# Context maxima of the next head pair: moved from four places in two units into four consecutive rounds of one unit

## The chip, the cores and the metric

The kernel runs on one core of a Trainium2 chip. The metric is the device time of one execution in microseconds (us), lower is better. All work is in one program; its stages follow one another with a barrier between them.

## The reference, cut to what matters

Two transformer layers over 1024 latent tokens and a prefix of 256 context tokens. In each layer 16 heads (8 of latent attention "MLA", 8 of grouped-query attention "GQA") attend; latent queries see all 1280 keys. In the first layer the context tokens attend too, over the 256 context keys alone; in the last layer they don't, since the context stream isn't used any more.

```python
o = jnp.concatenate([
    blocked_attention(qm, jnp.concatenate([kmc, km], axis=1),
                      jnp.concatenate([vmc, vm], axis=1), MLA_SCALE),
    blocked_attention(qg, jnp.concatenate([kgc, kg], axis=1),
                      jnp.concatenate([vgc, vg], axis=1), GQA_SCALE)], axis=-1)
x = layer_norm(ALPHA * x + ga * (o @ w_o[l]), ln1_g[l], ln1_b[l])
if not last:
    oc = jnp.concatenate([blocked_attention(qmc, kmc, vmc, MLA_SCALE),
                          blocked_attention(qgc, kgc, vgc, GQA_SCALE)], axis=-1)
# blocked_attention: softmax over the keys of q.k * scale, times v, per block of 128 queries
```

## The kernel before, in words

The function `attention` (L851) is one stage per layer. It walks through a list `U` of units. A unit is a pair of heads and a group of queries: (pair, first tile, tiles, key tiles). In the first layer each of the 8 pairs has three units: one context unit (2 query tiles, 2 key tiles), then two latent units (4 query tiles and all 10 key tiles each). Unit numbers run 0 to 23; units 0, 3, 6, ..., 21 are context units, 1, 4, ... are here called the first latent unit of a pair and 2, 5, ... the second. In the last layer there are no context units. Pairs 0 to 3 are MLA, pairs 4 to 7 GQA.

A unit works in rounds `k`, one for each key tile. In a round TensorE computes transposed scores (`scores`, L1096; keys on the partitions; 6 matmuls for MLA, 4 for GQA), ScalarE takes the exponential (`exponential`, L1177), and VectorE adds the result into a running sum (`accumulate`, L1233). The weighted values (`values`, L1123) are held back and issued in bunches: those of two rounds at k = 2, of three at k = 5, of three at k = 8, the last two at k = 0 of the next unit (`held`, L938).

The exponential needs the maximum of each query's row beforehand. It enters the scores as an extra row of the query operand, so it must be known before the unit begins. For each query tile and head of a *later* unit there is therefore an extra score matmul with the queries on the partitions, `begin(v, s)` (L1061), into a PSUM area, and VectorE takes the negated maximum of it (`maximum`, L1228, instruction L1231). For a latent unit that is 3 matmuls over 1280 keys and a reduction of 1280 columns; for a context unit one matmul over 256 keys and a reduction of 256 columns. A latent unit needs 8 of these, a context unit 4 (s = 0 to 3). When all are there, `turn(v)` (L1088) transposes the maxima, ScalarE copies them out (`take_row`, L1199) and SyncE's queue copies them into the query operand (`set_row`, L1011).

After the prologue all `begin`s share one PSUM area, `at_sc`: each waits until the maximum before it has been read out:

```python
if n >= PRO:
    pe.wait_ge(max_done, n)      # L1071, in begin; n is this begin's number in the whole order
```

In which round each `begin` is issued is written out by hand. `ahead(u, k)` gives those of later latent units: one in each round 0 to 5 and 8, 9. `context_ahead(u, k)` gives those of the next context unit: s = 0 and 1 in rounds 2 and 5 of the first latent unit before it, s = 2 and 3 in rounds 2 and 5 of the second. The order in a round on TensorE is: `scores(u, k)`, the `turn`s of `turned` (round 6), the `begin`s of `ahead`, the last values and sums of the unit before (rounds 0 and 1), the held `values`, and then the `begin` of `context_ahead` (L1155 to L1169). On VectorE it is: the maximum of `ahead`, `accumulate`, the maximum of `context_ahead`, and `invert` (L1255 to L1264). `invert(w)` takes the reciprocal of the softmax sums of an earlier unit, which went out to DRAM and came back by GpSimd's DMAs. TensorE and VectorE take their instructions in this written order.

The tables `begun`, `T_BEFORE`, `A_NO` (L913 to L924) follow from the two functions, so that both engines agree on the numbers to wait for. The maxima of the first two units of the stage are computed in its prologue and are in neither function.

Of the kernel before, what the change touches and what calls it, by code (L numbers as in the profile page):

```python
# [25 lines left out]
CT = CTX // P  # L26
LT = SEQ // P
NT = CT + LT
# [822 lines left out]
def attention(nc, S, C, layer):  # L851
# [17 lines left out]
    U = []  # L869
# [5 lines left out]
    LATENT = [u for u in range(len(U)) if U[u][3] == NT]  # L875
# [4 lines left out]
    def place(u):  # L880
        return U[u] + (U[u][2] * P,)

    def ahead(u, k):

        if U[u][3] != NT:
            return []
        n = LATENT.index(u)
        if k < 6 and n + 1 < len(LATENT):
            return [(LATENT[n + 1], k + 2)]
        if k >= 8 and n + 2 < len(LATENT):  # L890
            return [(LATENT[n + 2], k - 8)]
        return []

    def context_ahead(u, k):

        if U[u][3] != NT or k not in (2, 5):
            return []
        for v, half in ((u + 2, 0), (u + 1, 2)):
            if v < len(U) and U[v][3] == CT:
                return [(v, half + (k == 5))]  # L900
        return []

    def turned(u, k):

        if U[u][3] != NT:
            return []
        n = LATENT.index(u)
        if k == 6 and n + 1 < len(LATENT):
            return ([u + 1] if U[u + 1][3] == CT else []) + [LATENT[n + 1]]
        return []  # L910

    early = [0, 1] if first_layer else [0]
    begun = [(v, s) for v in early for s in range(2 * U[v][2])] + [(LATENT[1], s) for s in range(2)]  # L913
    T_BEFORE = {(v, s): early.index(v) for v in early for s in range(2 * U[v][2])}
    T_BEFORE.update({(LATENT[1], s): len(early) for s in range(2)})
    turns = list(early)
    for u in range(len(U)):
        for k in range(U[u][3]):
            turns += turned(u, k)
            begun += ahead(u, k) + context_ahead(u, k)  # L920
            T_BEFORE.update({vs: len(turns) for vs in ahead(u, k) + context_ahead(u, k)})
    A_NO = {vs: n for n, vs in enumerate(begun)}
    T_NO = {v: n for n, v in enumerate(turns)}
    assert len(A_NO) == len(begun) == sum(2 * unit[2] for unit in U) and len(T_NO) == len(U)  # L924
# [21 lines left out]
    with ExitStack() as cx:  # L946
# [35 lines left out]
        def score_bank(n):  # L982

            return st[:, :, :, :].rearrange("p b h n -> p (b h n)") if n < PRO and n % 2 else sc
# [75 lines left out]
        def _(pe):  # L1060
            def begin(v, s):  # L1061

                pair, t0, na, kb, nq = place(v)
                a, h, n = s // 2, s % 2, A_NO[v, s]
                if s == 0:
                    pe.wait_ge(q_loaded[v % QR][0], 16 * (v // QR + 1))
                    if pair < G0:
                        pe.wait_ge(k_loaded[pair % 2][0], 16 * (pair // 2 + 1))
                    else:
                        pe.wait_ge(g_loaded[0], 16)  # L1070
                if n >= PRO:  # L1071
                    pe.wait_ge(max_done, n)
                elif n >= 2:
                    pe.wait_ge(max_done, n - 1)
                bank = score_bank(n)
                if T_BEFORE[v, s]:
                    pe.wait_ge(nm_out, T_BEFORE[v, s])
                if pair < G0:
                    qq, kk = q[0:QK, v % QR, 0, a, h, :], km[0:QK, pair % 2, 0, h, :]
                else:  # L1080
                    qq, kk = q[:, v % QR, 0, a, h, :], kg[:, (pair - G0) // 2, :]
                for lo, hi in SC:
                    if lo < kb * P:
                        hi = min(hi, kb * P)
                        ins = nc.tensor.matmul(bank[:, lo:hi], qq, kk[:, lo:hi], start=True, stop=True)  # L1085
                ins.then_inc(a_full, 1)

            def turn(v):  # L1088

                na = U[v][2]  # L1090
                pe.wait_ge(max_done, A_NO[v, 2 * na - 1] + 1)
                if T_NO[v]:
                    pe.wait_ge(nm_out, T_NO[v])
                nc.tensor.transpose(sc[0:2 * na, 1280:1408], nm[:, v % 3, 0:2 * na], C["ident"][:, :]).then_inc(nm_full, 1)
# [28 lines left out]
            def values(u, k):  # L1123

                pair, t0, na, kb, nq = place(u)
                j = AT[u] + k
                if j == 0:
                    pe.wait_ge(v_loaded, 16)
                if k == 0 and u > 0:
                    pe.wait_ge(den_taken, u)  # L1130
                pe.wait_ge(exp_done, j + 1)
                for h in range(2):
                    col = 2 * pair + h if pair < G0 else H_MLA + (pair - G0) // 2
                    ins = nc.tensor.matmul(op[VD * h:VD * h + VD, 0:nq], va[:, k, col * VD:(col + 1) * VD],  # L1134
                                           pt[:, j % PT, h, 0:nq], start=(k == 0), stop=(k == kb - 1))
                ins.then_inc(v_done, 1)

            def sums(u):

                nq = U[u][2] * P  # L1140
                pe.wait_ge(acc_done, sums_done(u))
                pe.wait_ge(op_taken, u + 1)
                for h in range(2):
                    ins = nc.tensor.matmul(op[VD * h:VD * h + VD, 0:nq], C["ones"][:, 0:VD], acc[:, u % 2, h, 0:nq], start=True, stop=True)
                ins.then_inc(r_full, 1)
# [8 lines left out]
            for u in range(len(U)):  # L1154
                for k in range(U[u][3]):  # L1155
                    scores(u, k)
                    for v in turned(u, k):
                        turn(v)
                    for v, s in ahead(u, k):
                        begin(v, s)  # L1160
                    if k == 0 and u > 0:
                        for i in range(U[u - 1][3] - 2, U[u - 1][3]):
                            values(u - 1, i)
                    if k == 1 and u > 0:
                        sums(u - 1)
                    for i in held(u, k):
                        values(u, i)
                    for v, s in context_ahead(u, k):
                        begin(v, s)  # L1169
            u = len(U) - 1  # L1170
            for i in range(U[u][3] - 2, U[u][3]):
                values(u, i)
# [53 lines left out]
        @block.vector  # L1226
        def _(dve):
            def maximum(v, s):  # L1228
                kb = U[v][3]
                dve.wait_ge(a_full, A_NO[v, s] + 1)  # L1230
                nc.vector.tensor_reduce(nm[:, v % 3, s:s + 1], score_bank(A_NO[v, s])[:, 0:kb * P], AX.X, ALU.max, negate=True).then_inc(max_done, 1)  # L1231

            def accumulate(u, k):  # L1233
                nq = U[u][2] * P
                j = AT[u] + k
                out = acc[:, u % 2, :, 0:nq]
                dve.wait_ge(exp_done, j + 1)
                if k == 1:
                    if u >= 2:
                        dve.wait_ge(r_full, u - 1)  # L1240
                    before = pt[:, (j - 1) % PT, :, 0:nq]
                else:
                    dve.wait_ge(acc_done, sums_done(u - 1) + k - 1)
                    before = out
                nc.vector.tensor_tensor(out, before, pt[:, j % PT, :, 0:nq], ALU.add).then_inc(acc_done, 1)  # L1245

            def invert(u):

                dve.wait_ge(dc_loaded, 16 * (u + 1))
                n = 2 * U[u][2] * P // RC  # L1250
                nc.vector.reciprocal(rc[0:n, u % 2, :], dc[0:n, u % 2, :]).then_inc(inv_done, 1)

            for v, s in begun[:PRO]:
                maximum(v, s)
            for u in range(len(U)):  # L1255
                for k in range(U[u][3]):
                    for v, s in ahead(u, k):
                        maximum(v, s)
                    if k > 0:
                        accumulate(u, k)  # L1260
                    for v, s in context_ahead(u, k):
                        maximum(v, s)
                    for w in inverted(u, k):
                        invert(w)  # L1264
            u = len(U) - 1
            nq = U[u][2] * P
            dve.wait_ge(r_full, u + 1)
            dve.wait_ge(ot_ready, u - 1)
            nc.vector.reciprocal(rinv[:, u % 2, 0:nq], op[:, 0:nq]).then_inc(inv_done, 1)
            dve.wait_ge(inv_done, u + 1)  # L1270
            dve.wait_ge(op_taken, u + 1)
            dve.wait_ge(o_stored[u % 2], 16 * (u // 2))
            dve.wait_ge(ot_ready, u)
            nc.vector.tensor_tensor(ot[:, u % 2, 0:U[u][2], :].rearrange("p a n -> p (a n)"), raw[:, u % 2, 0:nq],
                                    rinv[:, u % 2, 0:nq], ALU.mult).then_inc(ot_ready, 1)
# [1026 lines left out]
```

## Time and profile before

| what | value |
|---|---|
| time, median of 3 runs | 3781.95 us (3776.68 to 3788.75) |
| the profiled execution's own time | 3788.75 us |
| its span in the profile | 3787.0 us |
| attention stage of the first layer | from about 445 us to 999 us of the span |
| granted TensorE clock, mean | 0.936 of full speed |

The profile is a page with the busy time of each engine, a strip of the span in 40 slices, the DMA queues, the chain that ended last, and the costliest groups of instructions. Besides it the trace can be asked for waits, for instructions in order of time, and for the busy time of chosen stretches. PE is TensorE's matmul row, PEld its weight loads; a row of PE that isn't idle can still be a matmul draining, because ends of matmuls are modelled. The start of a weight load (PEld) is the better mark of when TensorE came to the next piece of work.

### The profile page before, as it was taken

The numbers are of one execution on the slowest core, as the hardware profiler recorded it, in microseconds if no ns is written. First come the engines' busy times: TensorE is split into PE (matmuls) and PEld (weight loads), VectorE is DVE, ScalarE is ACT, GpSimd is POOL, SyncE is SP. The second block draws the span as 40 slices with busy tenths as digits, with TensorE's granted clock in tenths as the row PEclk, the third lists the DMA queues.
The fourth block names the chain that finished last, engine by engine and source line by source line (L and its number), as shares of the span: only waits on it lengthen the run. The fifth ranks groups of instructions, "written<-read, shape, count | busy, mean of one in ns | idle before, by whom it ended". The sixth has DMA issues, their size and how long they took to land. (4 is left out here: it accounts for less than half of the span.)

```text
span 3787.0 us, 44337 instructions
## 1 busy us (share of the span) xinstructions
PE 3304.8 (87%) x14416; PEld 2224.1 (59%) x14416; DVE 2715.6 (72%) x2841; ACT 1853.9 (49%) x2125; POOL 1456.2 (38%) x1091
## 2 busy tenths in 40 slices
PE   6999699999695999999959996999978599999990
PEld 2555355544384788888824443555437488887870
DVE  1444466677586899989856654777767698988997
ACT  0222233344310888888823332333331188888881
POOL 2111011121111877777721110111121287777771
PEclk9999799999896999999979997999999699999995
DMA  8465532211441998798754336221115278997974
GB/s 339 157 233 186 157 94 67 58 48 37 143 150 71 404 365 309 275 350 321 298 210 135 124 102 181 73 64 43 40 39 196 98 292 336 349 363 284 353 276 195
DMA packets 258758, 739.56 MB, mean 195 GB/s; under 512 B 55456, under 2 KB 149440, under 8 KB 205272
## 3 DMA queue, kind: packets, MB, share of 16 engines
q0 software_dynamic: 114288, 528.57, 36.4%
q1 hardware_dynamic: 129816, 157.73, 13.7%
q10 hardware_dynamic: 14544, 51.92, 3.8%
q8 instruction: 53, 0.87, 0.1%
q14 instruction: 57, 0.47, 0.0%
HBM read 723.62 MB, written 129.61 MB: 225 GB/s over the span
## 5 line engine op out<-in xcount | busy, mean ns | idle before, releaser
L2033 DVE TENSOR_TENSOR ex_wl<-ex_wr,ex_wh 128x2048 fp32r<-128x2048 f32 x440 | 988.0, 2285 | 63.9 <-ACT ex_wh L1978 63.8
L1978 ACT ACTIVATE ex_wh<-ex_wr 128x2048 fp32r<-128x2048 f32 x440 | 843.1, 1916 | 77.4 <-PE ex_yp L1941 55.1
L1185 ACT ACTIVATE at_pt<-at_st 128x1024 f32<-128x1024 f32 (+1 forms) x336 | 336.5, 1003 | 552.7 <-PE at_st L1120 550.0
L1231 DVE TENSOR_REDUCE at_nm<-at_sc 128x1 f32<-128x1280 f32 (+1 forms) x276 | 378.3, 1371 | 216.1 <-PE at_sc L1085 213.6
L764 PE MATMUL zp<-w_in,hT 128*128 128x480 f32 x960 | 428.8, 580 | 31.5 <-DVE hT L539 21.6
L1245 DVE TENSOR_TENSOR at_acc<-at_acc,at_pt 128x1024 f32<-128x1024 f32 x256 | 318.2, 1243 | 94.6 <-ACT at_pt L1185 92.4
L1859 POOL DMA_INDIRECT ex_wr<-in_w_down,piece_of x152 | 315.6, 2077 | 46.3 <-issue 46.0
L1134 PE MATMUL at_op<-at_pt,at_va 128*64 128x512 f32 (+1 forms) x1344 | 318.6, 603 | 0.2
L1120 PE MATMUL at_st<-at_q,at_km 96*128 96x512 f32 (+3 forms) x1008 | 266.2, 404 | 16.6 <-DMA at_q<-at_nmT 14.6
L764 PEld LDWEIGHTS zp<-w_in,hT 128*128 128x128 f32 x960 | 173.5, 195 | 180.2 <-issue 168.5
L1120 PEld LDWEIGHTS at_st<-at_q,at_km 96*128 96x128 f32 (+1 forms) x1008 | 180.6, 193 | 104.0 <-issue 42.6
L1879 POOL DMA_INDIRECT y_s<-ex_y,row_to x72 | 192.8, 2677 | 120.2 <-ACT ex_y L1986 117.3
L1918 PE MATMUL ex_gp<-ex_wh,ex_xh 128*128 128x512 f32 x576 | 226.7, 394 | 13.3 <-DVE ex_wl L2033 13.3
L1859 POOL DMA_INDIRECT ex_wr<-in_w_gate,piece_of x152 | 219.7, 1445 | 46.5 <-issue 46.5
L1936 PE MATMUL ex_yp<-ex_wh,ex_hh 128*128 128x512 f32 x576 | 233.3, 405 | 0.1
L1937 PE MATMUL ex_yp<-ex_wl,ex_hh 128*128 128x512 f32 x576 | 228.7, 397 | 0.0
L1919 PE MATMUL ex_gp<-ex_wl,ex_xh 128*128 128x512 f32 x576 | 226.2, 393 | 0.0
L1920 PE MATMUL ex_gp<-ex_wh,ex_xl 128*128 128x512 f32 x576 | 225.3, 391 | 0.0
L1920 PE MATMUL ex_vp<-ex_wh,ex_xl 128*128 128x512 f32 x576 | 224.3, 389 | 0.0
L1918 PE MATMUL ex_vp<-ex_wh,ex_xh 128*128 128x512 f32 x576 | 224.1, 389 | 0.0
L1919 PE MATMUL ex_vp<-ex_wl,ex_xh 128*128 128x512 f32 x576 | 224.1, 389 | 0.0
L1852 POOL DMA_INDIRECT ex_xb<-h_s,row_from x76 | 197.2, 2595 | 24.3 <-issue 22.5
(281 smaller groups left out, 5941.2 us busy)
## 6 DMA issues: line engine op xcount, KB each, us to landing
ad_w<-in_w_ada POOLq DMA_DIRECT2D x48, 1024.0 KB, 10.4
q_mla<-qT SPq DMA_DIRECT2D x40, 384.0 KB, 3.8
k_mla<-kT SPq DMA_DIRECT2D x40, 384.0 KB, 5.7
at_km<-k_mla SPq DMA_DIRECT2D x16, 960.0 KB, 12.0
at_q<-q_mla SPq DMA_DIRECT2D x32, 384.0 KB, 11.6
w_in<-in_w_in SPq DMA_DIRECT2D x6, 1920.0 KB, 25.5
q_gqa<-gqT SPq DMA_DIRECT2D x20, 512.0 KB, 6.8
cy<-y_s POOLq DMA_DIRECT2D x10, 1024.0 KB, 7.1
```

The costliest lines, as they stand in the source:

```text
L764: ins = nc.tensor.matmul(zp[:, n, 0:ZW], hT[:, k, :], w_in[:, k, n * ZW:(n + 1) * ZW], start=(k == 0), stop=(k == KC - 1))
L1120: ins = nc.tensor.matmul(st[:, j % 2, h, 0:nq], kk, qq, start=(m == 0), stop=(m == len(passes) - 1))
L1134: ins = nc.tensor.matmul(op[VD * h:VD * h + VD, 0:nq], va[:, k, col * VD:(col + 1) * VD], pt[:, j % PT, h, 0:nq], start=(k == 0), stop=(k ...
L1185: nc.scalar.activation(pt[:, j % PT, :, 0:nq], st[:, j % 2, :, 0:nq], ACT.Exp).then_inc(exp_done, 1)
L1231: nc.vector.tensor_reduce(nm[:, v % 3, s:s + 1], score_bank(A_NO[v, s])[:, 0:kb * P], AX.X, ALU.max, negate=True).then_inc(max_done, 1)
L1245: nc.vector.tensor_tensor(out, before, pt[:, j % PT, :, 0:nq], ALU.add).then_inc(acc_done, 1)
L1859: pool.indirect_dma_start(wr[:, u, p].rearrange("p a n -> p (a n)"), None, w, bass.IndirectOffsetOnAxis(R["wi"][:, p % 2, b:b + 1], 0), bo ...
L1918: nc.tensor.matmul(out[:, :], xh[:, k, :], wh[:, q, j, :], start=(k == 0), stop=False)
L1919: nc.tensor.matmul(out[:, :], xh[:, k, :], wl[:, q, j, :], start=False, stop=False)
L1920: ins = nc.tensor.matmul(out[:, :], xl[:, k, :], wh[:, q, j, :], start=False, stop=(k == KC - 1))
L1978: nc.scalar.activation(wh[:, q], wr[:, u, p], ACT.Copy).then_inc(hi_done, 1)
L2033: nc.vector.tensor_tensor(wl[:, q], wr[:, u, p], wh[:, q].bitcast(F32), ALU.subtract).then_inc(lo_done, 1)
```

## The change

`context_ahead` and its two loops go. `ahead` now also gives the context unit's `begin`s: in rounds 2, 3, 4, 5 of the second latent unit of a pair, s = 0, 1, 2, 3 of the context unit that follows, each right behind the latent `begin` of the same round. On VectorE the context maximum comes right behind the latent one and ahead of `accumulate`. There are seven such context units (3, 6, ..., 21) with 28 `begin`s and 28 maxima; nothing is added or removed in number. The last layer's attention has no context unit and the same order as before.

```diff
         n = LATENT.index(u)
         if k < 6 and n + 1 < len(LATENT):
-            return [(LATENT[n + 1], k + 2)]
+            return [(LATENT[n + 1], k + 2)] + ([(u + 1, k - 2)] if k >= 2 and U[u + 1][3] == CT else [])
         if k >= 8 and n + 2 < len(LATENT):
             return [(LATENT[n + 2], k - 8)]
-        return []
-
-    def context_ahead(u, k):
-
-        if U[u][3] != NT or k not in (2, 5):
-            return []
-        for v, half in ((u + 2, 0), (u + 1, 2)):
-            if v < len(U) and U[v][3] == CT:
-                return [(v, half + (k == 5))]
         return []
...
-            begun += ahead(u, k) + context_ahead(u, k)
-            T_BEFORE.update({vs: len(turns) for vs in ahead(u, k) + context_ahead(u, k)})
+            begun += ahead(u, k)
+            T_BEFORE.update({vs: len(turns) for vs in ahead(u, k)})
...
                     for i in held(u, k):
                         values(u, i)
-                    for v, s in context_ahead(u, k):
-                        begin(v, s)
...
                     if k > 0:
                         accumulate(u, k)
-                    for v, s in context_ahead(u, k):
-                        maximum(v, s)
                     for w in inverted(u, k):
                         invert(w)
```

## Rows read from the trace of the kernel before

**Rows 1.** The page: busy time, share, count of each engine; clock in 40 slices.

```profile
PE 3304.8 (87%) x14416; PEld 2224.1 (59%) x14416; DVE 2715.6 (72%) x2841; ACT 1853.9 (49%) x2125; POOL 1456.2 (38%) x1091
...
PEclk9999799999896999999979997999999699999995
```

**Rows 2.** Waits, 500 to 995 us: total us, times, longest.

```profile
ACT at_pt L1185 <- PE at_st L1120: 263.8, 148, 7.4
...
DVE at_nm L1231 <- PE at_sc L1085: 81.1, 68, 2.8
...
PE at_sc L1085 <- DVE at_nm L1231: 15.4, 32, 1.4
```

**Rows 3.** Timeline, second latent unit of an MLA pair (unit 5), rounds 2 to 6.

```profile
585.46 0.65 PEld L1085 LDWEIGHTS at_sc<-at_km,at_q 96*128 96x128 f32 x3
...
586.35 1.94 PE L1134 MATMUL at_op<-at_pt,at_va 128*64 128x512 f32 x8
586.46 1.49 DVE L1231 TENSOR_REDUCE at_nm<-at_sc 128x1 f32<-128x1280 f32 x1 [0.56 <-PE at_sc L1085]
...
588.22 0.19 PEld L1085 LDWEIGHTS at_sc<-at_km,at_q 96*128 96x128 f32 x1 [0.81 <-DVE at_nm L1231]
...
589.61 0.64 PEld L1085 LDWEIGHTS at_sc<-at_km,at_q 96*128 96x128 f32 x3
...
592.14 0.53 PEld L1085 LDWEIGHTS at_sc<-at_km,at_q 96*128 96x128 f32 x3 [0.60 <-DVE at_nm L1231]
...
592.72 1.24 PEld L1120 LDWEIGHTS at_st<-at_q,at_km 97*128 97x128 f32 x6
593.14 1.48 DVE L1231 TENSOR_REDUCE at_nm<-at_sc 128x1 f32<-128x1280 f32 x1
594.54 1.21 DVE L1245 TENSOR_TENSOR at_acc<-at_acc,at_pt 128x1024 f32<-128x1024 f32 x1
594.67 0.53 PEld L1085 LDWEIGHTS at_sc<-at_km,at_q 96*128 96x128 f32 x3 [0.71 <-DVE at_nm L1231]
...
598.19 0.19 PEld L1085 LDWEIGHTS at_sc<-at_km,at_q 96*128 96x128 f32 x1 [0.81 <-issue]
...
598.30 1.23 PEld L1120 LDWEIGHTS at_st<-at_q,at_km 97*128 97x128 f32 x6
598.62 0.42 DVE L1231 TENSOR_REDUCE at_nm<-at_sc 128x1 f32<-128x256 f32 x1 [0.33 <-PE at_sc L1085]
...
599.58 0.08 PEld L1094 LDWEIGHTS at_sc<-c_ident,at_nm 128*4 128x4 f32 x1
```

**Rows 4.** Timeline, second latent unit of a GQA pair (unit 14), rounds 2 to 6.

```profile
789.02 0.66 PEld L1085 LDWEIGHTS at_sc<-at_kg,at_q 128*128 128x128 f32 x3
...
795.48 0.53 PEld L1085 LDWEIGHTS at_sc<-at_kg,at_q 128*128 128x128 f32 x3 [1.08 <-DVE at_nm L1231]
...
801.62 0.19 PEld L1120 LDWEIGHTS at_st<-at_q,at_kg 128*128 128x128 f32 x1
...
802.44 0.09 PEld L1094 LDWEIGHTS at_sc<-c_ident,at_nm 128*4 128x4 f32 x1
```

**Rows 5.** Timeline, first latent units (units 7, 13), around round 3.

```profile
629.39 0.85 PE L1085 MATMUL at_sc<-at_km,at_q 96*128 96x512 f32 x3 [1.39 <-DVE at_nm L1231]
...
763.12 0.42 DVE L1231 TENSOR_REDUCE at_nm<-at_sc 128x1 f32<-128x256 f32 x1
...
763.59 0.84 PE L1085 MATMUL at_sc<-at_kg,at_q 128*128 128x512 f32 x3
```

**Rows 6.** Stretches of one unit (4, 7, 14, 17): us, busy times, PEclk.

```profile
549.34:581.12 31.78, 30.50 (x132) 17.98 (x133) 24.07 (x22) 11.14 (x13) 7.05 (x12) 1.00 0.33 80
...
617.58:652.92 35.34, 33.62 (x132) 18.78 (x133) 23.70 (x22) 11.14 (x13) 6.82 (x12) 0.90 0.32 76
...
785.59:813.78 28.19, 25.59 (x110) 13.56 (x111) 21.73 (x19) 11.34 (x14) 4.47 (x8) 1.00 0.13 36
847.72:877.46 29.74, 27.11 (x110) 14.18 (x111) 21.84 (x19) 11.35 (x15) 4.68 (x8) 0.94 0.10 28
```

## The prediction, made before the changed kernel was run

> **What bounds the kernel now.** I read the page first. TensorE is the busiest engine, VectorE the second [rows 1], but that is an average over stages, and the change touches one stage only, the first layer's attention (445 to 999 us). So the waits of that stage come next [rows 2]: ScalarE waited 263.8 us for scores and VectorE 81.1 us for TensorE, while matmuls of `begin` waited 15.4 us in all for VectorE. TensorE therefore sets the pace of the stage, and every microsecond in which it stands still there is lost. Then the timeline of a second latent unit, the place of the change, in an MLA pair [rows 3] and in a GQA pair [rows 4]. I call the latent `begin` of round k A(k) and a context `begin` B.
>
> The reader should see two things there. First, one score area is handed back and forth: from A(4)'s weight load at 592.14 VectorE starts its reduction 1.00 later (593.14), needs 1.48, and A(5) loads 0.05 behind its end, at 594.67. So **two `begin`s in a row cannot stand closer than 2.53 us** when the first is a latent one, whatever else TensorE has to do. In rounds 3 and 4 of the MLA unit that loop is already the pace (592.14 to 594.67, with scores between them that fill only part of it). Second, in rounds 2 and 5 B costs nearly nothing, because the held values stand between A and B: A(2) loads at 585.46, the reduction runs from 586.46 to 587.95, and meanwhile TensorE works on values from 586.35 until B loads at 588.22. B itself takes 0.11 of TensorE (598.19 to 598.30) and 0.42 of VectorE.
>
> **The change part by part.** It removes no instruction and adds none, and moves no DMA: 28 Bs, each one matmul over 256 keys, are issued elsewhere. 14 leave the first latent units; 14 stay in the second ones but in front of the values; so all 28 now stand right behind an A and wait for its reduction. Behind the waiting B on TensorE's queue stand the held values in rounds 2 and 5 and the next round's scores in rounds 3 and 4; ScalarE waits for those scores. SyncE's queue of row copies waits for the `turn` in round 6, which only moves with the rest; GpSimd's chain of sums goes on during the stalls and comes out no later.
>
> *MLA-type second units (2, 5, 8, 11; four).* From A(2) to the `turn` in round 6 now: 585.46 to 599.58, 14.12 us [rows 3]. In the changed order:
> - Round 2: A and its wait 2.53, B 0.11, then the values. These take 588.22 − 585.46 − 0.65 (A's own loads) = 2.11 with the gap ahead of them. Sum 4.75, where it is 2.87 now (585.46 to 588.33): +1.88.
> - Rounds 3 and 4: 2.53 + 0.11 + scores 1.28 (598.30 to 599.58) = 3.92 against 2.53: +1.39 each. B's reduction is through 0.43 + 0.42 + 0.05 = 0.90 after B's load (598.19 to 598.62, then 0.42) [rows 3], under the scores' 1.28, so A(k+1) doesn't wait for it.
> - Round 5: values and gap 598.19 − 594.67 − 0.64 = 2.88; 2.53 + 0.11 + 2.88 = 5.52 against 3.63: +1.89.
>
> Together +6.55 a unit, **26.2 us** for four.
>
> *GQA-type second units (14, 17, 20; three).* The span from A(2) to the `turn` is 789.02 to 802.44, 13.42 us [rows 4]. Scores take 0.82 (801.62 to 802.44). In the changed order: round 2 2.53 + 0.11 + 2.11 + 0.82 = 5.57; rounds 3 and 4 2.53 + 0.11 + 0.82 = 3.46, but VectorE has reduction 1.48, B's latency and reduction 0.85 and `accumulate` 1.21 in a row, which makes the next reduction about 0.1 late, so 3.55; round 5 2.53 + 0.11 + 2.88 + 0.82 = 6.34. Sum 19.0, +5.6 a unit, **16.8 us** for three.
>
> *First latent units (seven).* Each loses two Bs, 14 × 0.11 = 1.5 us. In the three GQA ones A(3) now stands behind B's reduction (763.12 + 0.42, A at 763.59 [rows 5]); that wait goes too, some 0.33 each, 1.0 in all. **−2.5 us**. In the MLA ones VectorE waits in round 2 for the sums that a DMA brings back (`invert`), which is what keeps A waiting 1.39 in unit 7 [rows 5]; there the 0.11 of round 2 may not be seen, at most 0.4 us less gain.
>
> *Cover of what I cost at nothing.* `accumulate` now comes behind B's reduction, some 0.8 later in each of the four rounds; the exponential that needs its buffer back is eight rounds on, and VectorE waits for TensorE in this stage anyway [rows 2]. Were that cover gone, it would cost 28 × 0.8 = 22 us; the GQA rounds, where it is thinnest, gave the 0.1 above.
>
> Subtotal 26.2 + 16.8 − 2.5 = **40.5 us**.
>
> *The clock.* The trace of before doesn't show this pattern, so I bound it. The granted TensorE clock is not 1 in all of the stage: unit 17 ran at 0.94 and took 29.74 us where its twin, unit 14, took 28.19 at 1.00; unit 7 at 0.90 took 35.34 where unit 4 took 31.78 at 1.00 [rows 6]. 0.94 means that some 2 × 0.06 × 29.74 = 3.6 us ran at 1.2 instead of 2.4 GHz; that fall cost 1.55 us. Unit 7's, twice as long, cost at most 3.56, part of which is its longer wait. The fall in unit 7 came behind an idle TensorE of 1.39 us [rows 5]. In the changed order TensorE is without a matmul for 2.53 less the 0.85 to 0.97 that A's matmuls show, about 1.6 us, four times within some 17 us. From below: no fall, 0. From above: two short falls or a long one in each of the seven units, 7 × 3.3 less the one that unit 17 has already, 22 us. I take one short fall a unit, which is nearest to units 7 and 17: 7 × 1.55 − 1.55 = **9.3 us**.
>
> The Trainium skill bears on this term ("TensorE: Matmul & The Clock Gate", section "A second HAM failure mode: psum-queue depth-cycling"): a kernel whose TensorE idles briefly and often while it hands PSUM areas round can swing between the two clock levels without any long gap. By that rule the clock term is wanted, and the sum is 50 or more; without it the sum is 40.5. The traces agree as far as unit 17 goes, which fell with short waits only, while unit 14 with the same order did not.
>
> Sum 40.5 + 9.3 = 49.8, about **+50 us**. The profiled execution took 3788.75 (span 3787.0); it lies 6.8 above the median of the three. The stage is followed by barriers and the rest is untouched, so the same 50 go on the median: 3781.95 + 50 = **3832 us** (3839 for an execution as slow as the profiled one). A difference under 0.3%, 11 us, can't be told from none here.
>
> **The rivals.**
> 1. *The waits alone, the clock holds.* For it: unit 14, with idle stretches in rounds 4 and 5 (PEld idle 1.08 in its row [rows 4]), kept 1.00. Against: unit 17. 3781.95 + 40.5 = 3822 us.
> 2. *The clock falls twice or for long in each second unit.* For it: four long stalls in one unit, where unit 7 fell for long after one of 1.39. 3781.95 + 40.5 + 22 = 3844 us.
> 3. *The waits are covered.* If the values or scores behind B went ahead of it, or TensorE's later waits shrank by as much, only the savings of the first units would be left: within 0.3%, 3779 to 3790 us. For it: in GQA rounds A waits for VectorE already, so part of TensorE's time there is free; I have counted that (rounds 3 and 4 cost 1.0, not 1.9). Against: A(5) itself stood waiting at 594.67 with PEld idle [rows 3] while the values of rounds 2 and 3 stood behind it, their exponentials done, and they didn't pass it. The Trainium skill says the same of the order (page above, "Step-by-step: what each phase is for"): only weight loads are pulled ahead, matmuls stay in program order.
> 4. *Faster, by the first latent units.* Without B, VectorE is less crowded in round 2, where unit 7 lost 3.56 to a wait and a low clock [rows 5, 6]. If this took away that fall, unit 17's and one like it at the stage's end, it would give 3.56 + 2 × 1.55 + 2.5, about 9 us: 3773 us. It decides only if a B in its new place costs under 9/28, 0.3 us, against the 1.4 to 1.9 worked out above.
>
> **How the numbers follow.** Forecast (one short fall a unit, 3826 to 3838) 0.45; rival 1 0.28; rival 2 0.17; rival 3 0.06; rival 4 0.04. The forecast and rivals 1 and 2 are all slower: 0.90, same 0.06, faster 0.04. The range goes from rival 1, 3822, less 6 for the spread of the runs and 4 for places where a stall hides a later wait, 3812, to rival 2, 3844, plus the 7 by which the slowest run shown lies above the median, 3851. The likeliest case's own range lies inside it.
>
> **What would show it right or wrong.** In the changed profile's second latent units each single-matmul `begin` should load about 2.53 us behind the three-matmul one ahead of it, with PEld idle some 1.9 and VectorE's reduction named. A to A in rounds 3 and 4 should be 3.9 (MLA) and 3.5 us (GQA); A(2) to `turn` 20.7 and 19.0. The total of `at_sc` matmuls waiting for `at_nm` should rise from 15.4 to some 55 us. First latent units should be 0.2 to 0.6 us shorter. The granted clock over the second units should be about 0.94; at 1.00 rival 1 has it, at 0.88 rival 2. The forecast is wrong in kind if the waits at B are there and the stage's end doesn't move.

## The result and the profile after

The changed kernel took 3839.3 us (median of 4 runs, 3836.8 to 3849.42), the kernel before beside it 3782.77 us. The ratio is 1.0164, 95% interval [1.0145, 1.0182]: 56.5 us by the medians, 62 by the ratio. It is slower, as forecast, by somewhat more than the 50 us forecast. The record lists 24 executions of the changed kernel in all; their median is 3844.3 us, which fits the 62. The profiled execution took 3847.76 us with a span of 3846.0.

Where the time went is read from four stretches that are the same pieces of work in both kernels. Columns: stretch, length, busy times of PE, PEld, DVE, ACT and POOL, granted clock, DMA. First the kernel before:

```profile
0.00:481.74 481.74, 404.99 (x1928) 215.13 (x1929) 190.32 (x410) 116.94 (x254) 69.70 (x85) 0.93 0.62 214
481.74:993.53 511.79, 481.31 (x2051) 265.40 (x2051) 359.73 (x319) 198.50 (x241) 96.43 (x161) 0.99 0.21 55
993.53:2384.60 1391.07, 1204.70 (x5056) 873.18 (x5056) 1044.93 (x1155) 748.01 (x852) 638.35 (x396) 0.92 0.64 235
2384.60:3787.00 1402.40, 1213.81 (x5384) 870.36 (x5383) 1120.59 (x958) 790.47 (x779) 651.73 (x449) 0.93 0.53 201
```

and the changed kernel:

```profile
0.00:480.63 480.63, 406.23 (x1928) 215.69 (x1929) 190.45 (x410) 116.91 (x253) 69.57 (x85) 0.89 0.62 215
480.63:1054.63 574.00, 506.02 (x2051) 278.25 (x2051) 362.25 (x319) 198.37 (x241) 99.08 (x161) 0.93 0.19 49
1054.63:2443.30 1388.67, 1203.11 (x5056) 870.22 (x5057) 1045.13 (x1155) 747.89 (x852) 638.10 (x396) 0.93 0.64 235
2443.30:3846.00 1402.70, 1212.31 (x5383) 869.22 (x5383) 1123.74 (x958) 790.11 (x779) 647.33 (x449) 0.93 0.53 201
```

The second stretch, units 1 to 23 of the first layer's attention, grew by 62.2 us with the same counts; the others moved by 3 us in all. In that stretch the granted clock fell from 0.99 to 0.93. It was lower in the first stretch too (0.89 against 0.93), but that stretch didn't get longer (480.63 against 481.74 us); there the low clock cost nothing.

The waits of the stage name the place (500 to 1045 us; total, times, longest). The third line, 15.4 us before [rows 2], is the one forecast at some 55:

```profile
ACT at_pt L1174 <- PE at_st L1111: 317.4, 147, 9.0
...
DVE at_nm L1220 <- PE at_sc L1076: 115.9, 94, 4.1
...
PE at_sc L1076 <- DVE at_nm L1220: 55.2, 46, 1.9
```

The timeline of unit 5 answers to [rows 3]:

```profile
596.53 0.65 PEld L1076 LDWEIGHTS at_sc<-at_km,at_q 96*128 96x128 f32 x3
...
597.53 1.49 DVE L1220 TENSOR_REDUCE at_nm<-at_sc 128x1 f32<-128x1280 f32 x1 [0.56 <-PE at_sc L1076]
599.25 0.19 PEld L1076 LDWEIGHTS at_sc<-at_km,at_q 96*128 96x128 f32 x1 [2.07 <-issue]
599.28 0.36 PE L1076 MATMUL at_sc<-at_km,at_q 96*128 96x256 f32 x1 [1.79 <-DVE at_nm L1220]
...
599.56 3.53 PE L1125 MATMUL at_op<-at_pt,at_va 128*64 128x512 f32 x8
...
604.36 0.65 PEld L1076 LDWEIGHTS at_sc<-at_km,at_q 96*128 96x128 f32 x3
...
605.36 1.49 DVE L1220 TENSOR_REDUCE at_nm<-at_sc 128x1 f32<-128x1280 f32 x1 [4.13 <-PE at_sc L1076]
606.91 0.19 PEld L1076 LDWEIGHTS at_sc<-at_km,at_q 96*128 96x128 f32 x1 [1.90 <-DVE at_nm L1220]
...
608.29 0.65 PEld L1076 LDWEIGHTS at_sc<-at_km,at_q 96*128 96x128 f32 x3
```

The context `begin` (the load "x1") now stands 2.55 us behind the latent one in round 3 (604.36 to 606.91) with PEld idle 1.90, and A(3) to A(4) is 3.93, forecast 3.92. In round 2 the distance is 2.72. Look at the values behind it: 8 matmuls in 3.53 us, where the same 8 took 1.94 [rows 3]. TensorE was at half clock there.

So two things make up the loss, and single units show both. First unit 8 of the kernel before, then three second units of the changed kernel (5, 8 and 14):

```profile
652.92:684.29 31.37, 29.68 (x130) 17.26 (x131) 21.52 (x19) 11.42 (x15) 4.85 (x8) 1.00 0.18 51
...
592.19:632.00 39.81, 32.03 (x132) 18.01 (x133) 22.86 (x21) 11.41 (x14) 4.87 (x8) 0.96 0.12 30
672.52:710.70 38.18, 30.37 (x132) 17.77 (x133) 22.93 (x21) 11.41 (x14) 4.79 (x8) 1.00 0.15 43
821.52:861.73 40.21, 32.44 (x112) 16.91 (x113) 22.50 (x21) 11.34 (x15) 5.47 (x8) 0.79 0.08 21
```

Unit 8 held its clock and is 38.18 us long; it was 31.36 (31.37 in the line, by rounding of its ends). Unit 14 at 0.79 is 12.0 longer than the 28.19 of [rows 6].

### The profile page after: what moved, and what is told of

Read it like the earlier page. It is cut to its first block and busy times, and to the rows that moved or that the text cites. A ratio compares the mean times of both kernels' runs of the same rounds, so it can differ in the third digit from the quotient of the medians.

```text
span 3846.0 us, 44337 instructions
## 1 busy us (share of the span) xinstructions
PE 3327.7 (87%) x14416; PEld 2233.4 (58%) x14416; DVE 2721.6 (71%) x2841; ACT 1853.3 (48%) x2125; POOL 1454.1 (38%) x1091
## 5 line engine op out<-in xcount | busy, mean ns | idle before, releaser
L1125 PE MATMUL at_op<-at_pt,at_va 128*64 128x512 f32 (+1 forms) x1344 | 327.4, 618 | 0.2
L1907 PE MATMUL ex_vp<-ex_wh,ex_xl 128*128 128x512 f32 x576 | 224.6, 390 | 0.0
```

The source lines that it names most:

```text
L1907: ins = nc.tensor.matmul(out[:, :], xl[:, k, :], wh[:, q, j, :], start=False, stop=(k == KC - 1))
```

## The experiments

A unit's length below is the time from the copy of the sums' raw values (`take_values`) in its round 0 to that in the next unit. The time at half clock is read from the granted clock of those stretches: 0.96 over 39.81 us is 2 × 0.04 × 39.81, about 3. The second units of the table include the last one, unit 23 (20.9 us before, 20.8 changed), which has no begins of a later unit.

| sums over the stage, us | second units (at half clock) | first units (at half clock) | stage |
|---|---|---|---|
| before | 232.3 (3.5) | 245.8 (10.2) | 511.8 |
| changed | 300.3 (68.3) | 239.9 (6.8) | 574.0 |
| changed_again | 297.8 (61.4) | 242.6 (6.8) | 574.1 |
| four_rounds_behind_values | 266.8 (44.4) | 246.5 (17.3) | 547.0 |
| old_rounds_right_behind | 267.3 (23.9) | 283.0 (34.1) | 584.0 |
| context_first | 271.7 (30.7) | 237.4 (0.0) | 542.8 |
| filled_stalls | 274.9 (0.0) | 240.5 (6.8) | 549.2 |
| half_filled_stalls | 274.9 (0.0) | 239.1 (0.9) | 547.8 |
| values_spread | 231.2 (0.0) | 238.7 (0.0) | 503.6 |
| spread_and_moved | 224.6 (0.0) | 254.4 (17.1) | 512.7 |
| values_spread_again | 231.4 (0.3) | 242.5 (5.0) | 507.5 |
| spread_moved_mended | 224.7 (0.0) | 236.7 (0.0) | 495.1 |

### Is it the place in the round, or four begins in one unit?

**old_rounds_right_behind** keeps the old rounds and units and moves only the place:

```diff
-                    for v, s in ahead(u, k):
+                    for v, s in ahead(u, k) + context_ahead(u, k):
                         begin(v, s)
...
-                    for v, s in context_ahead(u, k):
-                        begin(v, s)
```

(the same on VectorE with `maximum`).

> The kernel before with one thing changed: each context begin of rounds 2 and 5 stands right behind the latent begin, ahead of the values, and its reduction ahead of accumulate. Rounds and units are those of before. Theory (position): 28 covered begins become 28 uncovered ones, 14 x 1.89 in round 5, 8 x 1.88 and 6 x 1.5 in round 2 = 50 us, of which up to 3 are swallowed by the wait for the returned sums in the first MLA units; plus 5 to 20 us of low clock: +52 to +67, near 3842. Rival (crowding into rounds 3 and 4): no change, 3783.

It took 3858.1 us, ratio 1.0194 [1.0177, 1.0211] with 3782.03 before, 76 us by the medians: slower than the changed kernel, with no context begin in rounds 3 and 4 at all. The rival is out. Unit 11, without a clock fall, was 3.82 us longer than before (31.18; 3.77 expected from 1.88 and 1.89):

```profile
760.74:795.74 35.00, 30.00 (x128) 17.15 (x129) 21.55 (x19) 11.43 (x14) 5.10 (x8) 1.00 0.14 38
```

The edit moves the begin on TensorE and its maximum on VectorE together; no run moves one alone. The total is above the expected range, and 58 us of the stage were at half clock.

**four_rounds_behind_values** does the opposite: the rounds of the change, the old places.

```diff
     def context_ahead(u, k):
-        if U[u][3] != NT or k not in (2, 5):
-            return []
-        for v, half in ((u + 2, 0), (u + 1, 2)):
-            if v < len(U) and U[v][3] == CT:
-                return [(v, half + (k == 5))]
+        if U[u][3] == NT and k in (2, 3, 4, 5) and u + 1 < len(U) and U[u + 1][3] == CT:
+            return [(u + 1, k - 2)]
         return []
```

> As changed in where the 28 context begins are issued (rounds 2 to 5 of the second unit), but each stands behind the held values of its round, and its reduction behind accumulate. Theory (the cost is the wait of a begin right behind a latent one): rounds 2 and 5 are covered by values again and cost as before; rounds 3 and 4 have no values, A to A is 2.53 + 1.1 (accumulate) + 0.42 + 0.05 = 4.1 us against 2.53, +1.56 for 14 rounds = 22 us, less 4.3 us saved in the first units, plus one short clock fall in each unit at most (9 us): 18 to 27 us over the kernel before, near 3805. Rival (it is the crowding of four begins into one unit, whatever stands between): +50 to +60, near 3839.

It took 3821.81 us, ratio 1.0096 [1.0077, 1.0115]. Unit 14, at full clock, was 31.00 us, 2.81 over before, where 3.12 was expected; rounds 3 and 4 measured 3.88 from A to A, not 4.1. With rounds 2 and 5 covered, the loss of a GQA unit falls from 5.67 (filled_stalls, below) to 2.81; rounds 3 and 4 have no values to cover their begins and keep it. The rest of the miss is the clock: 62 us of the stage at half where some 9 us of loss had been allowed for, 44 of them in second units, each time behind one of the waits that are left (TensorE idle 1.58 us). Some are in first units that this kernel doesn't load more than the one before (unit 4 fell, 35.12 us). Unit 14:

```profile
812.00:843.00 31.00, 26.31 (x112) 13.78 (x113) 22.56 (x21) 11.34 (x14) 4.87 (x8) 1.00 0.12 29
```

**context_first** swaps the two begins of a round of the changed kernel, so that the second waits for the short reduction:

```diff
-            return [(LATENT[n + 1], k + 2)] + ([(u + 1, k - 2)] if k >= 2 and U[u + 1][3] == CT else [])
+            return ([(u + 1, k - 2)] if k >= 2 and U[u + 1][3] == CT else []) + [(LATENT[n + 1], k + 2)]
...
-                pe.wait_ge(max_done, A_NO[v, 2 * na - 1] + 1)
+                pe.wait_ge(max_done, A_NO[v, 2 * na - 1] + 1 + (U[v][3] == CT and v > 0))
```

> The changed kernel with the order of the two begins in a round swapped: context first, latent second (the turn of the context unit waits for one more reduction). Theory: the second begin now waits for a reduction of 256 columns (0.43 + 0.42 + 0.05 = 0.90) instead of 1280 (2.53). Rounds 2 and 5 +0.79, rounds 3 and 4 A to A 3.43 instead of 3.93 (MLA) and 3.55 (GQA), +0.90 over before: 7 x 3.38 = 24 less 4.3 = +19 us, plus low clock in the GQA units (0 to 10): 3802 to 3812. Rival (any second begin in a round costs the same hand-over): 3839.

3818.93 us, ratio 1.0096 [1.0079, 1.0113]: 20 us better than the changed kernel, but 37 over before and not the 20 to 30 expected. Unit 2, at full clock, is 4.46 longer than before, not 3.38. The timeline of its rounds 3 and 4 shows what I had left out:

```profile
523.67 0.53 PEld L1076 LDWEIGHTS at_sc<-at_km,at_q 96*128 96x128 f32 x3 [0.84 <-DVE at_nm L1220]
...
525.97 1.22 DVE L1234 TENSOR_TENSOR at_acc<-at_acc,at_pt 128x1024 f32<-128x1024 f32 x1
526.11 0.19 PEld L1076 LDWEIGHTS at_sc<-at_km,at_q 96*128 96x128 f32 x1 [0.60 <-DVE at_nm L1220]
...
527.10 0.42 DVE L1220 TENSOR_REDUCE at_nm<-at_sc 128x1 f32<-128x256 f32 x1
527.57 0.53 PEld L1076 LDWEIGHTS at_sc<-at_km,at_q 96*128 96x128 f32 x3 [1.28 <-DVE at_nm L1220]
```

By [rows 3] the context scores should be there 0.43 behind 526.11, but their reduction stands behind `accumulate` of the round before and starts at 527.10. A to A is 3.90, as in the changed kernel; only rounds 2 and 5 are cheaper.

### What is the clock's share?

**filled_stalls** leaves the waits and takes away the idleness: six score matmuls whose result the next round overwrites, in the wait of each of the 28 rounds.

```diff
-                    for v, s in ahead(u, k):
+                    for i, (v, s) in enumerate(ahead(u, k)):
+                        if i == 1:
+                            fill(u, k, 6)
                         begin(v, s)
...
+            def fill(u, k, count):
...
+                pe.wait_ge(exp_done, j - 1)
...
+                for _ in range(count):
+                    nc.tensor.matmul(st[:, j % 2, 0, 0:nq], kk, qq, start=True, stop=True)
```

(`j` is the next round's number; `kk` and `qq` are the keys and queries of this round's first score pass.)

> The changed kernel with six extra matmuls of 512 columns (a score pass whose result is overwritten) on TensorE between the latent and the context begin of each such round: 6 x 0.21 = 1.3 us of work in a wait of 1.87, so it adds no time by itself. Theory (part of the loss is the clock that falls behind idle TensorE): the clock stays at 1.00 in all seven second units, each is then 6.8 (MLA) or 5.7 us (GQA) longer than in the kernel before, and the time is +38 us, near 3821, 18 below the changed kernel. Rival (the falls have another cause, or cost nothing because the stage waits for VectorE): clock and time as changed, near 3839.

Four of its second units (2, 8, 14, 17):

```profile
511.21:549.38 38.17, 35.93 (x156) 21.98 (x157) 22.67 (x21) 11.42 (x14) 4.37 (x7) 1.00 0.12 34
661.51:699.66 38.15, 35.91 (x156) 21.97 (x157) 22.97 (x21) 11.41 (x14) 4.89 (x8) 1.00 0.12 31
806.54:840.43 33.89, 31.61 (x136) 18.37 (x137) 22.36 (x21) 11.34 (x14) 6.08 (x8) 1.00 0.09 26
873.26:907.12 33.86, 31.63 (x136) 18.38 (x137) 22.33 (x21) 11.34 (x15) 6.08 (x8) 1.00 0.10 26
```

With 24 matmuls more in each, the unit at full clock is as long as it was without them (38.15 against 38.18), and all seven are at 1.00. Doing more work made the kernel 13 us faster by the medians, 3826.02 against 3839.3 (3821 expected), and this profile's stage 24.8 us shorter. The ratio to before is 1.0118 [1.0101, 1.0135], clear of the changed kernel's [1.0145, 1.0182]; with the clock held, the loss left is 44 us by the medians, 37 in the profiled stage, where 38 was expected. The difference of the second units, 300.3 − 274.9 = 25.4 us, over 68.3 us at half clock makes 0.37 us lost for each. It isn't 0.5, which matmuls alone would lose at half speed, because the round holds VectorE's reduction too: in unit 2 of the changed kernel A(4) to A(5) took 5.80 us at half clock against 3.93, and the reduction in it took 1.49 at either level.

**half_filled_stalls** has `fill(u, k, 3)`.

> filled_stalls with three extra matmuls in each wait instead of six: 0.64 us of the 1.87, so that TensorE is idle about 1.0 to 1.2 us there. Theory (the clock falls when the idle time gets as long as some 1.4 us): few or no falls in the seven second units, each at 38.2 (MLA) and 33.9 us (GQA) as with six. Rival (any repeated idle time makes it fall): half-clock time of the order of the changed kernel's, 68 us in these units.

In its one execution (3824.01 us) no second unit fell. Unit 2 and unit 14:

```profile
511.34:549.49 38.15, 33.15 (x144) 19.72 (x145) 22.78 (x21) 11.42 (x14) 4.37 (x7) 1.00 0.12 34
808.06:841.94 33.88, 28.82 (x124) 16.11 (x125) 23.45 (x21) 11.35 (x14) 5.09 (x8) 1.00 0.12 32
```

Half the filling was enough here. That doesn't show a limit in the idle time of one wait: unit 17 of the kernel before fell with waits of 0.65 and 0.74.

**changed_again** is the changed kernel with nothing changed.

> The changed kernel once more, for how its clock falls differ from one execution to the next. Theory: the second units again have 40 to 80 us at half clock, in other places; units without a fall take 38.18 us (MLA) and 33.9 us (GQA). Rival: the same units fall for the same time.

3849.7 us. Unit 5, which had fallen, held; unit 8, which had held, fell for some 17 us:

```profile
592.37:630.52 38.15, 30.38 (x132) 17.77 (x133) 22.87 (x21) 11.43 (x15) 4.62 (x8) 1.00 0.12 32
671.23:715.67 44.44, 36.67 (x132) 21.03 (x133) 22.64 (x21) 11.42 (x14) 5.24 (x8) 0.81 0.13 36
```

Again 297.8 − 274.9 = 22.9 us over 61.4 make 0.37. Units 2, 5, 8 and 14 changed their time at half clock (17.1 to 10.2, 3.4 to 0, 0 to 17.1, 17.1 to 3.4), while units 11, 17 and 20 had the same in both (10.2, 13.7 and 6.8), so the rival is half right. The sum hardly moved, as far as two executions can tell.

### Can the score area's hand-over be covered better?

In rounds 3 and 4 of the kernel before TensorE waits too, since no values stand there. **values_spread** is that kernel with

```diff
-        return {2: range(0, 2), 5: range(2, 5), 8: range(5, 8)}.get(k, range(0))
+        return {2: range(0, 1), 3: range(1, 2), 4: range(2, 3), 5: range(3, 5), 8: range(5, 8)}.get(k, range(0))
```

> The kernel before (context begins in its rounds and places), with the held values spread: one in rounds 2, 3 and 4 each, two in round 5, instead of two and three in rounds 2 and 5. Both layers. Theory (rounds 3 and 4 are paced at 2.53 us by the hand-over of the score area, with TensorE idle 0.6 us in MLA and 1.05 us in GQA, and a group of values costs 0.35 us of gaps): a gain of 2 x (0.6 - 0.35) = 0.5 us in an MLA latent unit and 2 x (1.05 - 0.35) = 1.4 us in a GQA one, 16 of each: -30 us less what the first layer's context begin of round 2, now covered by one value only (1.87 of 2.53), costs: 14 x 0.7 = 10 and more where its own reduction then delays the next begin. Net -10 to -20 in all, the last layer's attention 15 shorter. Rival (VectorE, 1.48 + 1.22 us a round, is the real limit there): no change in rounds 3 and 4, 3783 to 3793.

3767.17 us, ratio 0.996 [0.9947, 0.9974] with 3784.81 before. The last layer's units shrank from 31.36 to 31.03 (MLA; 0.5 expected, 0.33 measured) and from 28.51 to 27.30 (GQA; 1.4 expected, 1.21 measured), that layer's attention from 440.25 to 428.22. In the first layer the second MLA units got 0.32 to 0.35 longer (units 1 and 10 0.5): one value covers 1.87 of 2.53, and the context begin of round 2 waits again (TensorE without a matmul for 0.58 in unit 5), the very fault of the change in small. The GQA second units 14 and 20 got 0.37 and 0.33 shorter.

**spread_and_moved** puts the context begins, on top of that, where they are covered:

```diff
     def context_ahead(u, k):
...
-        for v, half in ((u + 2, 0), (u + 1, 2)):
-            if v < len(U) and U[v][3] == CT:
-                return [(v, half + (k == 5))]
+        for v, at in ((u + 2, {5: 0, 7: 1, 8: 2}), (u + 1, {5: 3})):
+            if k in at and v < len(U) and U[v][3] == CT:
+                return [(v, at[k])]
```

> As values_spread, and the context begins put where the order leaves room: s = 0, 1, 2 in rounds 5 (behind two values), 7 (no latent begin there) and 8 (behind three values) of the first unit, s = 3 in round 5 of the second. Theory (only what stands between a latent begin and a context one counts): each costs 0.11 us, so the full gain of the spreading stands in both layers, 25 to 32 us under the kernel before: 3751 to 3758. Rival (the first layer gains nothing, since VectorE limits it): -15.

3774.23 us, ratio 0.9979 [0.9967, 0.9992]: worse than values_spread. The second units did what was expected (30.94 and 26.65), the first ones got 0.9 to 4.0 us longer than in values_spread, five of the seven with a clock fall of 3.4 us. Unit 10 shows it (rounds 7 and 8):

```profile
711.79 0.19 PEld L1085 LDWEIGHTS at_sc<-at_kg,at_q 128*128 128x128 f32 x1 [0.23 <-issue]
...
713.09 1.23 DVE L1245 TENSOR_TENSOR at_acc<-at_acc,at_pt 128x1024 f32<-128x1024 f32 x1 [0.30 <-ACT at_pt L1185]
...
714.23 0.42 DVE L1231 TENSOR_REDUCE at_nm<-at_sc 128x1 f32<-128x256 f32 x1
714.87 0.53 PEld L1085 LDWEIGHTS at_sc<-at_kg,at_q 128*128 128x128 f32 x3 [1.71 <-issue]
714.90 0.82 PE L1085 MATMUL at_sc<-at_kg,at_q 128*128 128x512 f32 x3 [1.31 <-DVE at_nm L1231]
```

The scores loaded at 711.79 are not reduced until 714.23, because the reduction stands behind `accumulate(7)`, which waits for ScalarE; and the latent begin of round 8 waits for it. I had again counted the engine and not the order on it. **spread_moved_mended** has that one maximum ahead of `accumulate`:

```diff
+                    if k == 7:
+                        for v, s in context_ahead(u, k):
+                            maximum(v, s)
                     if k > 0:
                         accumulate(u, k)
-                    for v, s in context_ahead(u, k):
-                        maximum(v, s)
+                    if k != 7:
+                        for v, s in context_ahead(u, k):
+                            maximum(v, s)
```

> spread_and_moved with the context maximum of round 7 ahead of accumulate on VectorE. There it stood behind accumulate(7), which waits for ScalarE's exponential, and the latent begin of round 8 waited for it (first units 1.4 us and, with clock falls, 3 to 4 us longer than in the last layer). Theory: first units as in the last layer, about 31.3 us (MLA, units 4 and 7 up to 1 more for the returned sums) and 27.5 (GQA), second units as before the mending 30.9 and 26.6, no falls: first-layer stage about 492 us, 20 under the kernel before, with the last layer's 12 some 30 us in all: 3753. Rival (the moved begins hold the first units up in round 8 too): stage 500 or more, 3763 or more.

3758.64 us, ratio 0.9935 [0.9922, 0.9947] with 3782.15 before: 24 us under the kernel before and 81 under the changed one, the fastest here. The stage is 495.1 us (492 expected), no unit at half clock. Beside it, **values_spread_again** is values_spread with nothing changed:

> values_spread once more, beside it on the same chip: 3767 again (0.4% under the kernel before), so that the two can be set side by side.

3767.55 us, ratio 0.9959 [0.9947, 0.9971]; the two intervals just touch at 0.9947, and 9 us lie between the medians; the slowest execution of spread_moved_mended (3759.65) is faster than the fastest of this one (3766.45).

## Why the prediction was right, and where its sizes were off

**The bound and the mechanism: right.** The slowdown is in the stage named, TensorE stands at the context begins as forecast, and old_rounds_right_behind shows that it is their place and not their number in a unit. The signs named for the waits came: 55.2 us of waits for `at_nm` in all (55), A to A 3.93 (MLA) and, in unit 14 of filled_stalls, 3.53 (GQA; 3.5), A(2) to `turn` 20.9 in unit 8 (20.7).

**The waits in the second units: right, a little small.** Forecast 6.55 (MLA) and 5.6 us (GQA) a unit, 43.0 in all; filled_stalls, without falls, gives 38.16 − 31.36 = 6.80 and 33.86 − 28.19 = 5.67, so 4 × 6.80 + 3 × 5.67 = 44.2. Most of the missing 0.25 of an MLA unit is in round 2, where A to B took 2.72 and not 2.53.

**The first units: right as counted, with a wait beside it that varies.** Forecast −2.5. Units 1 and 10 got 0.21 shorter, as counted. Units 13, 16 and 19 got 1.02 to 1.12 us shorter (29.25 to 28.19, 29.33 to 28.21, 29.24 to 28.22), twice the 0.55 counted (0.22 for two begins, 0.33 for the wait behind B). Their rounds show that 0.52 to 0.55 of it is there by round 9. The other half lies in one wait behind that, of the next unit's first scores for its maxima, which SyncE's queue copies in. Unit 13 before, changed and in changed_again:

```profile
781.88 0.19 PEld L1120 LDWEIGHTS at_st<-at_q,at_kg 128*128 128x128 f32 x1 [1.47 <-DMA at_q<-at_nmT]
...
817.79 0.19 PEld L1111 LDWEIGHTS at_st<-at_q,at_kg 128*128 128x128 f32 x1 [0.95 <-DMA at_q<-at_nmT]
...
823.44 0.19 PEld L1111 LDWEIGHTS at_st<-at_q,at_kg 128*128 128x128 f32 x1 [1.58 <-DMA at_q<-at_nmT]
```

In changed_again, the same program, that wait is back at 1.58 and the unit is 28.84 long, 0.41 under before. So this half differs from one execution to the next, and that any of it is due to the change isn't shown. Unit 4 got 0.8 shorter and unit 7 0.1 longer; both wait for returned sums, and unit 4 took 32.21 in changed_again against 30.99 here. In all the first units give −4.4 in this profile without the last one, 22, which lost no begin; its 1.5 us are a clock fall that only the kernel before had.

**The clock: the term that was mis-sized.** I took "one short fall a unit", 9.3 us, as "nearest to units 7 and 17". Measured are 25.4 us in the second units of the profile, less the 1.5 of unit 17 before: 24, above my upper bound of 22. Per unit there were 0 to 17 us at half clock, not 3.6. The sign that I had named says the same: over the seven second units the granted clock was 1 − 68.3/(2 × 279.5) = 0.88, the value put down for rival 2, not the forecast's 0.94. I had put the price of one short fall on each unit, though four waits longer than the one that preceded the fall in [rows 5] stood in it. The price was near enough: 1.55 us for 3.6 is 0.43 for a microsecond at half clock, and 0.37 was measured. It was the number and the length of the falls. The Trainium skill ("TensorE: Matmul & The Clock Gate", section "A second HAM failure mode: psum-queue depth-cycling") says that a TensorE that idles briefly and often between groups of matmuls can swing between the two clock levels. The second units of filled_stalls agree: their waits are as long (A to B 2.54 and more), only the idleness is gone, and so are the 68.3 us at half clock.

Together in the profile: 44.2 − 4.4 + 24 − 1.5 (unit 22) = 62.3, the 62.2 measured for the stage. Rivals 1, 3 and 4 are out: the clock fell, and the waits weren't covered. The median of four, 3839.3, lies between the forecast and rival 2, just outside the 3826 to 3838 of the case held likeliest; the 62 by the ratio and the median of all 24 executions, 3844.3, are rival 2's figures (+62.5, 3844). So the direction, the place and the price of the waits were worked out rightly, and the total stayed in the range because rival 2 was in it; one short fall a unit was the wrong pick.

## What to carry to other kernels

Where two engines hand one buffer back and forth, count what stands in program order between two users of it, on both engines: a small task right behind a big one costs the big one's whole round trip (here 1.9 us for 0.11 us of work), and the same task behind 2 us of other work costs little more than its own 0.11. Count the waits of the *other* instructions on the reducing engine as well; twice here an `accumulate` in between made the hand-over late. Then ask what the repeated idleness does to TensorE's clock, and test it by filling the gap with throw-away matmuls: that tells the wait from the clock.

## What the runs showed of the hardware that I had not expected

- More matmuls made the kernel faster: 168 of 512 columns in the gaps took back some 25 us of 62 in the profiled stage, and 84 did as well in one execution.
- The same program fell to half clock in different units from one execution to the next (unit 8: 0 and 17 us), yet for about the same sum (68 and 61 us). A microsecond at half clock cost 0.37 us in both.
